# One burst for each group's norm pieces in layer 1 of a hybrid decoder step

## The chip, the cores and the metric

The kernel runs on one core of one Trainium2 chip. The metric is the device time of one execution in microseconds. Three runs of the kernel before gave 1513.77, 1514.11 and 1514.53 us (median 1514.11). Engines: PE is the matmul engine (PEld its weight loads), DVE the vector engine, ACT the scalar engine, POOL the GpSimd engine, SP the engine that issues most transfers.

## The reference

One inference step of two layers for a prompt of 1024 tokens with 16 meta tokens ahead of it and for 8 sample tokens. Model width is 1024. Layer 0 mixes tokens by gated linear attention (4 heads), layer 1 by a Mamba-2 scan (32 heads in 4 groups of B and C, a causal convolution over 4 rows). Each layer normalises its input, projects it, mixes, gates, projects back, normalises and adds:

```
for i in range(DEPTH):                       # DEPTH = 2
    h = rmsnorm(x, pre_norm[i])
    if i % 2 == 0: y, S = gla_mixer(h, ...)      # h @ w_in (1024 x 3088), chunked scan, @ w_out
    else:          y, S, buf = ssd_mixer(h, ...) # h @ w_in (1024 x 5152), conv, chunked scan, @ w_out
    x = x + rmsnorm(y, post_norm[i])
```

Everything is float32. The outputs are the two results and the new states.

## The kernel before

**Tiles.** The 1048 token columns are cut into nine steps: step 0 holds the 24 sample and meta columns, steps 1 to 8 hold 128 tokens each. Group 0 is steps 0 to 4, group 1 is steps 5 to 8. A layer's heads are cut into four units u. A matmul in float32 precision is made of three products of high and low halves, so each weight tile is converted twice: its high half by ACT (`high`, line 867 or 876), its low half by DVE (`low`, line 883 or 885).

**Two kinds of work.** The mixing of a unit's step (`distance`, `keys`, `levels`, `decay`, `state`, `attend`, `scale`, `products` and others in layer 0; `scan`, `gates`, `norm`, `inputs`, `products`, `sample` and others in layer 1) is a chain through PE, ACT and DVE. The projections of units to come are *pieces*: one piece is 24 matmuls (line 1482) over 268 or 512 columns, cut into four parts of six. A piece's bank is evacuated by ACT (`evac`) and emptied by DVE (`drain`) where two results are made from it. Pieces use three banks in turn: piece i waits until piece i - 3 has been drained.

**Norm pieces.** Before a group's first unit in a layer, the normalised rows must stand as columns in `h`. Each step of the group has two norm pieces, each with four transposes (line 1114). ACT writes the high half of `h` from the bank (line 1492), DVE the low half (line 1540). Before them stand `n_in` (the rows' load), `n_square` (ACT and POOL) and `n_scale` (DVE, line 1078). In layer 1, group 0 has ten norm pieces (108 to 117) and group 1 has eight (202 to 209). The next piece after them is a `low` one, which waits until the two banks before it are free.

**The order.** `Plan` writes one list of tasks, and every engine runs its own tasks of it in that order. `skeleton` lists the mixing steps with `fill` entries between them and a `mark` at each unit's first load. `fill_in` places the pieces: between two marks it takes the cost that has to be placed (`goal`), divides it by the sum of the fills and places parts until the spent cost reaches the due share (`pieces_to`). A piece costs its columns / 128; a norm piece costs 1.2. With a piece's first part go the `evac` of the piece before it and `finish`, `close` and `store` of earlier ones; with its second part the `drain` of the piece before it (`part`). In the order before, pieces 106 to 111 lie between mark 6 and mark 7 (unit (0, 1, 3)), 112 to 117 behind it. The steps around them are those of layer 0, group 1, units 1 and 2, as (u, s): a step is named here by the event whose `keys` it holds. Pieces 202 to 205 lie ahead of mark 11 (unit (1, 0, 3)) and 206 to 209 behind it, in the steps of layer 1, group 0, unit 2.

Of the kernel before, what the change touches and what calls it, by code (L numbers as in the profile page):

```python
# [94 lines left out]
class Piece:  # L95
# [18 lines left out]
    @property  # L114
    def cost(self):
        if self.tile >= 0:
            return CGS[self.g][1] / P
        return 1.2 if self.kind == "norm" else 0.6


class Plan:


    def __init__(self):
        self.pieces, self.tiles = [], []
        self.last = []
        self.early, self.low = {}, {}
        for L, G, u in UNITS:
            self.unit(L, G, u)
            self.last.append(len(self.pieces) - 1)  # L130
        self.first_of = {}
        self.last_of = {}
        for i, p in enumerate(self.pieces):
            if p.tile >= 0:
                self.first_of.setdefault(p.tile, i)
                self.last_of[p.tile] = i
        self.weights, self.order, self.lows = [], [], []
        self.at = (0, 0)
        self.fill_in(self.skeleton())

    def unit(self, L, G, u):
# [209 lines left out]
    def lag(self, i, names):  # L351
        if 0 <= i < len(self.pieces):
            for name in names:
                self.order.append((name, i))

    def store_lag(self, i):

# [48 lines left out]
        return whole + (self.pieces[i].cost * p / self.pieces[i].parts if p else 0.0)  # L406

    def pieces_to(self, cost):
        while self.at[0] < len(self.pieces) and self.spent(self.at) < cost - 1e-6:
            self.part()  # L410

    def goal(self, k):
        return self.spent((min(self.last[k] + 5, len(self.pieces)), 0))

    def fill_in(self, tasks):

        marks = [i for i, t in enumerate(tasks) if t[0] == "mark"]
        assert [tasks[i][1] for i in marks] == list(range(len(UNITS)))
        for i, task in enumerate(tasks):
            if task[0] == "mark":  # L420
                self.pieces_to(self.goal(task[1]))
                if task[1] + 1 < len(UNITS):
                    end = marks[task[1] + 1]
                    room = sum(t[1] for t in tasks[i:end] if t[0] == "fill")
                    base = self.spent(self.at)
                    rate = (self.goal(task[1] + 1) - base) / room
                    filled = 0.0
                else:
                    rate = 0.0
            elif task[0] == "fill":  # L430
                if rate:
                    filled += task[1]
                    self.pieces_to(base + rate * filled)
            elif task[0] == "weight":
                self.high(("out", task[1]))
            elif task[0] == "lows":
                self.low_now()
            else:
                self.order.append(task)


# [2347 lines left out]
```

## Time and profile before

| | |
|---|---|
| median of three runs | 1514.11 us |
| profiled execution | 1509.73 us |
| its span | 1508.0 us |
| mean granted PE clock | 0.983 |
| PE busy | 1416.8 us (94%) |
| DVE busy | 1166.0 us (77%) |
| ACT busy | 837.3 us (56%) |
| POOL busy | 241.6 us (16%) |

All rows come from the profiled execution. Times of rows are microseconds from the start of its span. A busy share is an average over stretches with different limits; PE's busy time counts a matmul that runs at half clock in full.

### The profile page before, as it was taken

The page shows a single profiled execution, that of the slowest core. Times are in us where ns is not written, and L with a number is a line of the kernel's source. Part 1 is how long each engine was busy: PE and PEld are TensorE (multiplying, and loading weights), DVE is VectorE, ACT ScalarE, POOL GpSimd, SP SyncE. Part 2 cuts the span into 40 slices and gives each one's busy share as a digit, 9 for nine tenths or more (in the row PEclk, how much of TensorE's full clock was granted, in tenths as well). Part 3 has the DMA queues.
Part 4 walks back from the last instruction along what each step waited for, and adds up shares of the span by engine and source line. Part 5 has one row for each costly group of instructions (what it writes and reads, how often), then busy time and mean ns, then how long its engine had stood idle before and what let it go on. Part 6 is the DMA issues. An engine that isn't in the chain of part 4 may idle for free. (4 is left out here: it accounts for less than half of the span.)

```text
span 1508.0 us, 31302 instructions
## 1 busy us (share of the span) xinstructions
PE 1416.8 (94%) x11554; PEld 1179.1 (78%) x11554; DVE 1166.0 (77%) x2591; ACT 837.3 (56%) x1877; POOL 241.6 (16%) x424
## 2 busy tenths in 40 slices
PE   5989999799999969999999999989999999999987
PEld 5889887667888759898888988867777777777765
DVE  4556587758877887968977898995889787588786
ACT  4745555356556545546655665664655556465453
POOL 5010122001332100012111112121011211000002
PEclk8999999999999999999999999999999999999999
DMA  6465557355585433448844764753485574555453
GB/s 191 126 217 145 173 171 220 96 164 165 150 202 182 128 117 108 140 107 214 251 128 125 237 200 145 212 160 98 144 264 163 152 212 131 161 155 174 139 190 63
DMA packets 283874, 245.77 MB, mean 163 GB/s; under 512 B 32664, under 2 KB 250876, under 8 KB 283052
## 3 DMA queue, kind: packets, MB, share of 16 engines
q1 hardware_dynamic: 273628, 209.36, 47.1%
q0 software_dynamic: 10096, 34.41, 8.7%
q8 instruction: 93, 1.52, 0.4%
q14 instruction: 57, 0.47, 0.1%
HBM read 183.02 MB, written 65.00 MB: 164 GB/s over the span
## 5 line engine op out<-in xcount | busy, mean ns | idle before, releaser
L1482 PE MATMUL bank<-h,w 128*128 128x268 f32 (+1 forms) x4752 | 834.9, 330 | 22.8 <-ACT w L867 16.0
L1482 PEld LDWEIGHTS bank<-h,w 128*128 128x128 f32 x4752 | 701.5, 192 | 100.4 <-issue 25.5
L883 DVE TENSOR_TENSOR w<-w_raw,w 128x1024 fp32r<-128x1024 f32 x132 | 160.9, 1219 | 37.7 <-ACT w L867 37.2
L852 PE MATMUL bank<-s_w_out,s_yt_hi 128*128 128x512 f32 (+2 forms) x544 | 168.1, 398 | 2.0 <-DVE s_ys L2600 1.7
L867 ACT ACTIVATE w<-w_raw 128x1024 fp32r<-128x1024 f32 x132 | 138.7, 1051 | 7.3 <-DMA w_raw<-in_ssd_w_in_dram 7.3
L1560 DVE SCALAR_TENSOR_TENSOR conv<-before_conv,cw,conv 128x260 f32<-128x260 f32 (+2 forms) x216 | 125.3, 580 | 4.3
L852 PEld LDWEIGHTS bank<-s_w_out,s_yt_hi 128*128 128x128 f32 (+2 forms) x544 | 95.9, 180 | 28.4 <-issue 2.5
L852 PE MATMUL bank<-g_w_out,g_ot_hi 128*128 128x512 f32 (+2 forms) x288 | 97.2, 426 | 1.1 <-DVE g_ot_lo L2118 0.9
L852 PE MATMUL bank<-s_w_out,s_yt_lo 128*128 128x512 f32 x240 | 94.7, 395 | 0.0
L2363 ACT ACTIVATE s_decay<-s_decay,t_ac 128x128 f32<-128x128 f32 (+1 forms) x288 | 85.5, 379 | 1.2
L1528 ACT ACTIVATE conv<-bank,cw 128x268 f32<-128x268 f32 (+1 forms) x72 | 45.8, 637 | 72.2 <-PE bank L1482 55.3
L2682 ACT ACTIVATE s_yt_hi<-bank 128x512 fp32r<-128x512 f32 (+1 forms) x36 | 20.1, 557 | 110.7 <-PE bank L2673 110.6
L1813 POOL TENSOR_SCALAR g_omean<-g_osum 128x1 f32<-128x1 f32 (+1 forms) x36 | 17.0, 471 | 387.2 <-ACT squares L2090 387.1
L2338 POOL TENSOR_SCALAR s_ymean<-s_ysum 128x1 f32<-128x1 f32 (+1 forms) x36 | 18.4, 510 | 363.9 <-ACT squares L2666 363.7
L2321 POOL DMA_DIRECT2D out_dram<-s_sample_state x32 | 25.1, 784 | 301.8 <-DVE s_sample_state L2475 301.8
L1632 DVE SCALAR_TENSOR_TENSOR stage<-stage,conv 128x268 f32<-128x268 f32 (+1 forms) x72 | 37.3, 519 | 41.5 <-ACT stage L1589 41.1
L852 PEld LDWEIGHTS bank<-g_w_out,g_ot_hi 128*128 128x128 f32 (+2 forms) x288 | 52.9, 186 | 18.9 <-DVE g_ot_lo L2118 2.9
L1851 ACT ACTIVATE g_decays<-g_decays 128x1024 f32<-128x1024 f32 (+1 forms) x36 | 35.2, 979 | 57.2 <-DVE g_decays L1839 57.2
L1901 ACT ACTIVATE g_vr_turned<-bank 128x512 f32<-128x512 f32 (+1 forms) x36 | 21.2, 590 | 73.7 <-PE bank L1889 73.7
L2563 PEld LDWEIGHTS bank<-s_xdt,s_decay 128*32 128x32 f32 (+1 forms) x2112 | 33.7, 109 | 27.3 <-issue 27.3
L1520 ACT ACTIVATE conv<-bank 128x268 f32<-128x268 f32 (+1 forms) x72 | 32.6, 453 | 38.8 <-PE bank L1482 34.4
L2175 DVE SCALAR_TENSOR_TENSOR y_acc<-bank,s_yrstd,y_acc 128x512 f32<-128x512 f32 (+1 forms) x54 | 39.2, 745 | 19.1 <-PE bank L852 19.0
(259 smaller groups left out, 2458.8 us busy)
## 6 DMA issues: line engine op xcount, KB each, us to landing
w_raw<-in_ssd_w_in_dram SPq DMA_DIRECT2D x80, 512.0 KB, 4.3
w_raw<-in_gla_w_in_dram SPq DMA_DIRECT2D x48, 512.0 KB, 4.5
s_decay<-kept_acd SPq DMA_DIRECT2D x32, 512.0 KB, 6.3
w_raw<-in_ssd_w_out_dram SPq DMA_DIRECT2D x30, 512.0 KB, 4.1
g_chunk<-kept_gq SPq DMA_DIRECT2D x32, 448.0 KB, 5.2
s_chunk<-kept_sq SPq DMA_DIRECT2D x32, 384.0 KB, 4.9
kept_sq<-stage SPq DMA_DIRECT2D x80, 134.0 KB, 4.4
kept_sq<-stage SPq DMA_DIRECT2D x40, 256.0 KB, 4.8
```

What stands on the lines that cost most here:

```text
L852: last = pe.matmul(bank[0:r, :], yt[a][:, k, 0:r], wo[:, b, 512 * half:512 * half + 512], start=(k + a + b == 0), stop=(k == tiles - 1 and ...
L867: act.activation(self.part(i, 0), self.raw(i), ACT.Copy).then_inc(self.w_hi, 1)
L883: dve.tensor_tensor(self.part(i, 1), self.raw(i), hi, ALU.subtract).then_inc(self.w_lo, 1)
L1482: last = pe.matmul(bank[:, 0:n], w[:, p.tile % 2, a, k, :], h[:, b, k, c:c + n], start=(i == 0), stop=(i == len(terms) - 1))
L1520: act.activation(self.work(i)[:, 0:n], bank[:, 0:n], ACT.Tanh, scale=0.5).then_inc(self.tanhed, 1)
L1528: act.activation(self.work(i)[:, 0:n], bank[:, 0:n], ACT.Identity, scale=m["cw"][:, 3, a:a + 1], bias=m["cw"][:, 4, a:a + 1])
L1560: return dve.scalar_tensor_tensor(out=u[:, off:n], in0=x[:, k:k + w], scalar=cw[:, k, a:a + 1], in1=u[:, off:n], op0=ALU.mult, op1=ALU.add)
L1632: dve.scalar_tensor_tensor(out=self.slot(i)[:, 0:n], in0=self.slot(i)[:, 0:n], scalar=1.0, in1=self.work(i)[:, 0:n], op0=ALU.add, op1=ALU. ...
L1851: act.activation(E, E, ACT.Abs).then_inc(self.dabs, 1)
L2175: return dve.scalar_tensor_tensor(out=y, in0=bank, scalar=rstd, in1=y, op0=ALU.mult, op1=ALU.add)
L2363: last = act.activation(L[0:n, r, :], L[0:n, r, :], ACT.Relu, scale=-1.0, bias=ac[0:n, s, h:h + 1])
L2563: last = pe.matmul(self.own(u, s)[rows, r * HD:(r + 1) * HD], G[0:n, r, rows], t["xdt"][0:n, r * HD:(r + 1) * HD], start=True, stop=True)
```

## The change

Norm pieces of layer 1 cost nothing in the planner. `pieces_to` stops in front of them. A new function `norms` places all norm pieces of a group one after another, and right behind them the `evac` and `drain` of the last one, which `lag` then leaves out in their old place. `fill_in` calls it at every mark and ahead of each step's first task (`distance` in layer 0, `decay` in layer 1), and it acts only when the next piece is a norm piece of layer 1. Layer 0's norm pieces keep cost and place.

```diff
     def cost(self):
         if self.tile >= 0:
             return CGS[self.g][1] / P
-        return 1.2 if self.kind == "norm" else 0.6
+        if self.kind == "norm":
+            return 0.0 if self.L else 1.2
+        return 0.6
...
+        self.drained = set()
...
     def lag(self, i, names):
         if 0 <= i < len(self.pieces):
             for name in names:
-                self.order.append((name, i))
+                if (name, i) not in self.drained:
+                    self.order.append((name, i))
...
     def pieces_to(self, cost):
-        while self.at[0] < len(self.pieces) and self.spent(self.at) < cost - 1e-6:
+        while self.at[0] < len(self.pieces) and self.spent(self.at) < cost - 1e-6 and not self.norm_next():
             self.part()
+
+    def norm_next(self):
+        p = self.pieces[self.at[0]]
+        return p.kind == "norm" and p.L == 1
+
+    def norms(self):
+
+        if self.at[0] == len(self.pieces) or not self.norm_next():
+            return
+        while self.norm_next():
+            self.part()
+        i = self.at[0] - 1
+        self.lag(i, ["evac", "drain"])
+        self.drained.update({("evac", i), ("drain", i)})
...
             if task[0] == "mark":
                 self.pieces_to(self.goal(task[1]))
+                self.norms()
...
             else:
+                if task[0] == "distance" or task[0] == "decay" and task[1] == 1:
+                    self.norms()
                 self.order.append(task)
```

## Rows read from the trace of the kernel before

**Rows 1.** The page: busy time by engine; a group: busy, mean ns, idle before.
```profile
PE 1416.8 (94%) x11554; PEld 1179.1 (78%) x11554; DVE 1166.0 (77%) x2591; ACT 837.3 (56%) x1877; POOL 241.6 (16%) x424
...
L883 DVE TENSOR_TENSOR w<-w_raw,w 128x1024 fp32r<-128x1024 f32 x132 | 160.9, 1219 | 37.7 <-ACT w L867 37.2
```

**Rows 2.** Windows of group 0's place: length, busy by engine, PE clock, DMA share, GB/s.
```profile
505.93:517.28 11.35, 11.35 (x105) 9.19 (x103) 10.49 (x25) 6.59 (x15) 2.59 (x5) 1.00 0.34 94
517.28:529.24 11.96, 10.96 (x99) 8.01 (x97) 11.10 (x26) 5.12 (x10) 0.74 (x2) 1.00 0.40 114
529.24:542.45 13.21, 8.02 (x92) 6.11 (x91) 12.34 (x27) 6.30 (x13) 1.91 (x2) 0.97 0.51 130
542.45:553.74 11.29, 8.74 (x91) 6.47 (x89) 9.26 (x26) 4.48 (x12) 0.74 (x2) 0.88 0.57 194
553.74:572.38 18.64, 14.39 (x124) 12.63 (x125) 14.25 (x32) 8.18 (x17) 0.74 (x2) 0.82 0.21 61
```

**Rows 3.** Waits of PE from 500 to 570 us: total, times, longest.
```profile
PE bank L1114 <- DVE h L1540: 5.1, 2, 3.8
PE bank L2072 <- DVE g_attn L1996: 3.4, 1, 3.4
PE bank L1482 <- ACT w L867: 1.6, 1, 1.6
```

**Rows 4.** Waits of PE from 960 to 1020 us, group 1's place.
```profile
PE bank L1482 <- ACT w L867: 3.9, 1, 3.9
PE bank L2553 <- issue: 2.5, 1, 2.5
```

**Rows 5.** Windows before and across group 1's norm pieces.
```profile
834.50:994.50 160.00, 154.40 (x1387) 134.89 (x1387) 145.14 (x366) 96.65 (x256) 30.42 (x48) 1.00 0.67 200
...
999.99:1024.68 24.69, 19.69 (x154) 15.45 (x154) 20.19 (x58) 14.26 (x43) 5.82 (x9) 0.93 0.37 97
```

**Rows 6.** Timeline of PE: start, duration, instruction, count, idle before and releaser.
```profile
496.32 4.44 PE L1482 MATMUL bank<-h,w 128*128 128x512 f32 x18
...
554.98 0.75 PE L1114 MATMUL bank<-ident,y_acc 128*128 128x128 f32 x4 [3.75 <-DVE h L1540]
...
560.73 1.04 PE L1114 MATMUL bank<-ident,y_acc 128*128 128x128 f32 x8
...
565.43 3.99 PE L1482 MATMUL bank<-h,w 128*128 128x268 f32 x18 [1.62 <-ACT w L867]
...
582.48 7.65 PE L1482 MATMUL bank<-h,w 128*128 128x268 f32 x60
```

**Rows 7.** Timeline of DVE in the same stretch.
```profile
537.07 1.28 DVE L885 SCALAR_TENSOR_TENSOR g_w_out<-w_raw,wn,g_w_out 128x1024 fp32r<-128x1024 f32 x1
...
562.41 1.89 DVE L1540 TENSOR_TENSOR h<-bank,h 128x512 fp32r<-128x512 f32 x3 [1.17 <-ACT h L1492]
```

**Rows 8.** Timeline of ACT: evacuations of norm pieces.
```profile
561.78 1.57 ACT L1492 ACTIVATE h<-bank 128x512 fp32r<-128x512 f32 x3
```

**Rows 9.** Timeline of PE at the kernel's start, layer 0's norm pieces.
```profile
11.82 1.97 PE L1114 MATMUL bank<-ident,y_acc 128*128 128x128 f32 x8 [3.07 <-DVE y_acc L1078]
...
20.38 1.97 PE L1114 MATMUL bank<-ident,y_acc 128*128 128x128 f32 x8 [2.27 <-DVE h L1540]
...
24.24 11.96 PE L1482 MATMUL bank<-h,w 128*128 128x268 f32 x75 [0.95 <-ACT cw L770]
```

**Rows 10.** Timelines of PE and DVE at the transposes of z.
```profile
1004.02 0.63 PE L2643 MATMUL bank<-ident,s_z 128*128 128x128 f32 x4 [0.45 <-DVE states L2588]
...
1006.31 1.28 DVE L1540 TENSOR_TENSOR h<-bank,h 128x512 fp32r<-128x512 f32 x2
```

**Rows 11.** The page's transfers: count, KB each, us from issue to landing.
```profile
s_decay<-kept_acd SPq DMA_DIRECT2D x32, 512.0 KB, 6.3
...
kept_sq<-stage SPq DMA_DIRECT2D x80, 134.0 KB, 4.4
```

## The prediction

> **What bounds the kernel now.** I read the page first: the matmul engine (PE) is busy for 94% of the span, the vector engine (DVE) for 77% [rows 1]. So time can only come from PE's idle 91 us and from stretches at the lower clock. Next, the windows cut at the steps' borders around group 0's norm pieces: five steps of layer 0 from 505.9 to 572.4 us, 66.5 us long [rows 2]. The reader is to compare the columns PE and DVE with the length. In the first both are full (11.35 and 10.5 of 11.35); in the next two DVE works 11.1 of 12.0 and 12.3 of 13.2 us and sets the length. In the last three PE works only 8.0, 8.7 and 14.4 us, because hardly anything but norm pieces is left to fill them, and the granted clock is 0.97, 0.88 and 0.82. PE's idle time over the five is 13.0 us; the clock adds (1 - clock) x length = 0.4 + 1.4 + 3.4, about 5 us. Third, what PE waited for there [rows 3]: norm transposes for drains (5.1), the attend matmul for DVE (3.4), the first projection after the norms (1.6; its last drain ended just before it). At group 1's place the first projection after the norms waited 3.9 and a scan 2.5 us [rows 4]; from 1000.0 to 1024.7 us PE idled 5.0, at a clock of 0.93, which is 1.7 more [rows 5]. The stake is 13 + 5 + 2.5 + 5 + 1.7 = 27 us at most. Outside these two places PE is nearly always full, and work brought forward out of those stretches is saved.
>
> **Where the pieces go.** I followed the planner's rules. A layer 1 norm piece now costs 0 instead of 1.2, so goals after each group's norms fall by 12.0 and then by 9.6 more. Between mark 6 and mark 7 the fills (24 of 0.5) have 8.0 to place instead of 12.8: one 512-column part (cost 1.0) on every third fill. The nine parts still open go 3, 2, 2, 2 over the four steps (before: 4, 3, 2, 0), and the last is placed before the last but one fill. Then the ten norm pieces stand ahead of the distance of the fifth step, with their n_scale, evacuations and drains. The next interval places 55.6 over 18.0 at a rate of 3.09 (before 3.49, of which 7.2 was for norms), so that fifth step gets 2.5 x 3.09 = 7.7, fifteen 268-column parts instead of 3. For group 1, 33.5 instead of 38.3 goes over 16.56: the last part falls in the last fill, and the eight norm pieces stand at the mark, after the transposes of z and ahead of the load for the last unit. The instructions themselves are all kept: 72 transposes, 18 evacuations, 18 drains, every weight load. Only their order changes, so this is all about waits. One more thing to read off: group 1's burst does not stand in front of a step but inside one, since its last part comes too late for the step's head.
>
> **Prices.** A 512-column part is 6 of the 18 matmuls that take 4.4 us: 1.42 us. A 268-column part is a tenth of the 60 that take 7.65: 0.75 us [rows 6]. A drain is 0.6 us (three in 1.89), an output weight's low half, and n_scale with it by its like size, 1.2 without the overlap of 0.08 [rows 7], an input weight's 1.1 [rows 1]; an evacuation 0.5 [rows 8]. A layer 0 step without extras costs DVE 9.1 us: the fourth window has 9.3 us of work, 0.9 of it drains, and each step has a wait of 0.7 for ACT that stays (10.5 of 11.35 filled) [rows 2]. For PE such a step is 11.45 - 4 x 1.42 = 5.8 us by the first window's length, in which it never idles.
>
> **Group 0.** DVE's extras per step, in the new order: 2.3 (n_scale, one low half), 0, 5.3 (n_scale, two output halves, one input half, one drain), 0. So DVE asks 11.4, 9.1, 14.4, 9.1. PE asks 5.8 + 2 x 1.42 = 8.6, and with the order of keys, parts and attend about 9.5 between two attends. The steps take 11.4 + 9.5 + 14.4 + 9.5 = 44.8, and 1.8 for the clock after the long wait that the third step leaves: 46.6 us. The third step is the weak place: nearly all extras meet in it, and PE will idle some 5 us there, as now.
>
> The burst: DVE is free about when PE is, because its add of the products ends 1 us after them and PE has a part in between. n_scale takes 1.2, the drain of piece 107 comes at +1.3, and the third norm piece needs that piece's bank. From there the drains follow at 0.6, two of them small. With three banks the round trip PE 0.5, ACT 0.5, DVE 0.6 and the handovers just fit. PE leaves the burst after 6.5 us, of which 4.3 are its own transposes: 2.2 us idle. The last two drains hide beneath keys and levels of the step (1.6 us), ahead of the low piece that waits for them. What queues behind the drains on DVE is the step's distance, 7 us late, and behind it ACT's decays. Its cover is fifteen parts, 11.3 us of PE work; without it the burst would cost those 7 us. So burst and step take 6.5 + 5.8 + 11.3 = 23.6, and 1.5 for the clock after the transposes. That last is a bound by a neighbour: the 18 matmuls after the present norms took 3.99 us where the rate of the 60 gives 2.3 [rows 6]. Zero would be the lower end, and the 2.3 us that the start of the kernel lost (75 in 11.96 instead of 9.6) the upper [rows 9].
> Sum: 46.6 + 23.6 + 1.5 = 71.7 us against 66.5, but with twelve more parts done, 9.0 us: a gain of 3.8, rounded to 4. Bounds: +9 if the third step's extras spread, -1 if the burst's round trips take 1.1 us each.
>
> **Group 1.** When PE has turned z (1004.0) DVE still has scan work until 1006.3 [rows 10]. The third norm piece waits for the drain of 201 behind it: idle 1.4. Then 1.1 in the round trips and 1.4 until the low piece's two drains: 3.9 us, in place of 7.1 (the scan's 2.5, and 5.0 of the window less 0.4 that stays) [rows 4, 5]. The clock loss stays. Against this stands that the parts moved here, eight of 0.75 us, come from earlier steps; from 834 to 994 us DVE works 145 of 160 us [rows 5], so about a third of these 6 us frees nothing there. Gain 7.1 - 3.9 - 2 = 1.2, taken as 1. Bounds: +4 if all of it is freed, -3 if the burst has the start's prices. The load of the last unit now waits for the store of piece 201, issued only inside the burst: 4.4 us, then 6.3 for the decay rows [rows 11], so these are there some 12 us after the burst begins to drain. ACT needs them after about 14 us. I take 0; if it is late, each us counts once.
>
> **The sum.** 4 + 1 = 5 us off the profiled execution's 1509.7 (span 1508.0): 1504.7. The median of the runs lies 4.4 us above that execution, at 1514.1, so I forecast 1509.0 us.
>
> **A rule against it.** At the kernel's start, where norm pieces run nearly alone, eight transposes take 1.97 us [rows 9]; at 560.7 us the same eight take 1.04 [rows 6]. The first are at 1.2 GHz, the second at 2.4, and what PE did before the first was to wait 2.3 us. The Trainium skill, "TensorE: Matmul & The Clock Gate", section "A second HAM failure mode: psum-queue depth-cycling", says that going round PSUM banks with many short idles can make the clock swing, and that throughput is lost between bursts though single matmuls look normal. The trace agrees in kind (clock 0.82 and 0.88). By that rule the burst is the wrong form; what it would do here is the second rival.
>
> **The rivals.**
> Nothing (24%): DVE bounds these steps and its work is unchanged. It works 57.4 of 66.5 us [rows 2]. PE's new parts then only push its idle time to the next step, and conv drains come onto DVE earlier. Gain of 0 to 3: about 1513.
> Slower (23%): the burst runs at the start's prices. From 11.8 to 22.3 us eight full norm pieces took 1.3 us each, mostly at 1.2 GHz [rows 9]. Then group 0's burst takes 8 x 1.3 + 0.9 = 11.3 instead of 6.5 (+4.8), group 1's 10.4 instead of 7.4 (+3.0), and each restart loses 0.7 more (+1.4): 9.2 against a gain of 5, so 1518. It decides from the point where the two bursts idle PE 5 us longer than the forecast's 2.2 and 3.9. For it: the present drains already hold PE up for 3.8 us at once (at 554.98) [rows 6]. Against it: that wait came because steps' work stood between the drains.
> More (11%): the third step's extras find room in the light steps beside it and both restarts keep the clock: +5 in group 0, +3 in group 1, 1501.
> Forecast (42%): its own range 1506 to 1511.
>
> **How the numbers follow.** A change of 0.2% (3 us) is about what can be told from none here. Faster takes nearly all of the forecast's 42% and the 11%: 0.51. Same takes the rest of these and most of the nothing case: 0.27. Slower: 0.22. The range 1502 to 1518 leaves out half of the large gain and the worst of the slower case.
>
> **What would show it.** In the new trace: nine 512-column parts spread 3, 2, 2, 2; ten norm pieces in one stretch of 6 to 7 us near 551 us, and eight in one of 7 to 8 near 1003; PE idle of 2 and 4 us in them; a wait of some 5 us on g_attn after the step with the output weights; the granted clock in the fifth step above 0.9. Wrong if a burst lasts over 10 us, if the step after it waits for distance, or if PE's idle only turns up in the steps ahead of the burst.

## The result, and the profile after: 0.65% slower

The changed kernel takes 1521.9 us (median of four runs, 1521.1 to 1523.4) against 1513.9: ratio 1.0065, 95% interval 1.0048 to 1.0082, so 7 to 12 us slower where 5 us faster was forecast. Measured again later (e15 below) it is 1.0065 again, 1.0051 to 1.0079. One execution of all, the profiled one of e5, ran at a granted clock of 0.75 and took 1743.3 us; it is left out.

The page of the changed kernel, answering to [rows 1]. Line numbers are those of before plus 21.

```profile
PE 1427.1 (94%) x11554; PEld 1184.5 (78%) x11554; DVE 1165.3 (77%) x2591; ACT 838.4 (55%) x1877; POOL 237.1 (16%) x424
...
L904 DVE TENSOR_TENSOR w<-w_raw,w 128x1024 fp32r<-128x1024 f32 x132 | 160.8, 1218 | 35.5 <-ACT w L888 35.0
```

The same 11554 matmuls keep PE busy for 10.3 us longer than before; PE's idle time in the span of 1521.6 us grew by 3.3 us, from 91.2 to 94.5. DVE does the same work. The mean granted clock is 0.976 where it was 0.983, and (1 - clock) x span is 36.5 us against 25.6, so in this execution the longer busy time is the lower clock. That is no fixed part of the loss: e15, the same kernel once more, has 5.6 us more busy and 4.6 us more idle time than before at a mean clock of 0.983, the same as before's. Both executions are slower than before by more than the medians are, since the profiled execution of the kernel before (1509.7) is a fast one.

Windows of the changed kernel around group 0's burst, one for each step of layer 0, cut where a step's first transposes of the values start on PE; columns as in [rows 2], whose cuts lie at other points of the steps, so that the rows are not to be compared one by one.

```profile
519.61:528.64 9.03, 8.94 (x92) 6.96 (x91) 8.18 (x25) 4.32 (x9) 0.99 (x2) 1.00 0.29 82
528.64:545.13 16.49, 11.88 (x93) 8.71 (x91) 14.35 (x30) 6.73 (x11) 0.74 (x2) 0.79 0.65 203
545.13:564.13 19.00, 17.18 (x162) 14.30 (x161) 15.90 (x35) 10.46 (x21) 1.06 (x2) 1.00 0.20 57
564.13:583.34 19.21, 19.21 (x188) 18.18 (x187) 14.25 (x43) 13.31 (x28) 0.74 (x2) 1.00 0.31 90
583.34:611.31 27.97, 24.13 (x250) 22.14 (x249) 23.85 (x63) 11.23 (x30) 1.99 (x2) 0.88 0.45 129
```

The third of these holds the burst: PE is busy for 17.2 of its 19.0 us at the full clock. The fourth is full. The fifth, the second step after the burst, is where it goes wrong: 28.0 us, with DVE at work for 23.9 of them and a clock of 0.88. The timeline of PE shows the burst itself (start, duration, instruction, count, idle before):

```profile
547.04 0.67 PE L1135 MATMUL bank<-ident,y_acc 24*128 24x24 f32 x8
548.52 1.53 PE L1135 MATMUL bank<-ident,y_acc 128*128 128x128 f32 x12 [0.81 <-DVE stage L1570]
550.59 1.85 PE L1135 MATMUL bank<-ident,y_acc 128*128 128x128 f32 x12 [0.54 <-DVE h L1561]
552.66 1.26 PE L1135 MATMUL bank<-ident,y_acc 128*128 128x128 f32 x8 [0.22 <-DVE h L1561]
```

It lasts 6.7 us (forecast 6.5) and PE idles 1.6 us in it (forecast 2.2). Group 1's burst in the same view, with the first projections behind it:

```profile
1010.51 0.60 PE L1135 MATMUL bank<-ident,y_acc 128*128 128x128 f32 x4
1012.30 1.60 PE L1135 MATMUL bank<-ident,y_acc 128*128 128x128 f32 x12 [1.19 <-DVE stage L1570]
1014.37 1.85 PE L1135 MATMUL bank<-ident,y_acc 128*128 128x128 f32 x12 [0.47 <-DVE h L1561]
1016.43 0.65 PE L1135 MATMUL bank<-ident,y_acc 128*128 128x128 f32 x4 [0.21 <-DVE h L1561]
1018.70 4.58 PE L1503 MATMUL bank<-h,w 128*128 128x512 f32 x12 [1.61 <-ACT w L888]
```

PE's waits in the changed kernel from 500 to 575 us, then from 575 to 640, then from 890 to 1110 us (columns as in [rows 3]):

```profile
PE bank L2093 <- DVE g_attn L2017: 4.7, 2, 3.8
...
PE bank L1135 <- DVE stage L1570: 0.8, 1, 0.8
PE bank L1135 <- DVE h L1561: 0.8, 2, 0.5
```

```profile
PE bank L1503 <- ACT t_ac L1359: 3.1, 1, 3.1
PE bank L1503 <- ACT w L888: 2.5, 1, 2.5
PE bank L1503 <- ACT before_conv L1553: 0.8, 1, 0.8
```

```profile
PE bank L2664 <- DVE states L2609: 4.5, 2, 2.9
PE bank L2574 <- issue: 3.9, 2, 2.8
PE bank L2664 <- DVE s_yt_lo L2712: 3.2, 1, 3.2
PE bank L1503 <- ACT w L888: 1.6, 1, 1.6
```

Of the 5.1 us on norm drains of [rows 3] 1.6 are left (both rows of L1135), and of the 3.9 of [rows 4] 1.6. The wait of a scan there has only moved: from 890 to 1110 us it was 4.6 us in all before and is 3.9 (L2574). New are t_ac (602 us), states (4.5 us ahead of group 1's burst, where before had 0.5) and s_yt_lo (1064 us, behind it).

To see where time is lost when the order of the work differs, I compare the two timelines at equal progress: the start of the same step on PE, less the projection work already done ahead of it (1.43 us per 512-column part, 0.43 us per norm piece). Positive is behind the kernel before:

| at (us of before) | 496 | 582 | 604 | 757 | 894 | 987 | 1034 | 1074 | end |
|---|---|---|---|---|---|---|---|---|---|
| changed | -1.0 | -7.0 | +1.0 | +4.8 | +4.8 | +11.5 | +7.3 | +13.7 | +13.3 |
| e15, changed again | -0.9 | -8.0 | +1.0 | +3.9 | +3.9 | +11.2 | +5.5 | +10.7 | +10.2 |
| e16, one evacuation | -0.2 | -7.3 | -4.3 | -0.3 | -0.3 | +6.4 | +2.3 | +8.6 | +8.4 |
| e3, old places | -1.8 | -4.0 | -2.5 | -2.2 | -2.2 | -1.0 | -5.0 | -5.0 | -4.5 |
| e12, rate behind group 1 | -1.2 | -3.6 | -3.6 | -1.6 | -1.6 | -0.3 | -2.6 | +2.6 | +3.0 |
| e7, thin before group 1 | -0.8 | -0.3 | -0.3 | +2.4 | +2.4 | +9.2 | +4.6 | +7.3 | +7.0 |
| e18, group 0's rates, one evacuation | -0.4 | -6.3 | -3.2 | -0.2 | -0.2 | +1.2 | -2.7 | -2.7 | -0.8 |

The changed kernel gains 6 us up to 582 and 4 from 987 to 1034: these are the bursts. It loses 8 from 582 to 604 and 4 more to 757, 7 from 894 to 987, and 6 from 1034 to 1074: these are stretches of projections. Each row is one execution, set against one execution of before that was 4 us faster than its median, so the last column runs high. e3, e7 and e12 have the same order up to 894 us and differ there by up to 4.6 us, so a step of this table under 3 us proves nothing, and the medians below decide.

### The profile page after: what moved, and what is told of

The parts are those of the page before. It is cut to its first block and busy times, and to the rows that moved or that the text cites. A ratio compares the mean times of both kernels' runs of the same rounds, so it can differ in the third digit from the quotient of the medians.

```text
span 1521.6 us, 31302 instructions
## 1 busy us (share of the span) xinstructions
PE 1427.1 (94%) x11554; PEld 1184.5 (78%) x11554; DVE 1165.3 (77%) x2591; ACT 838.4 (55%) x1877; POOL 237.1 (16%) x424
## 5 line engine op out<-in xcount | busy, mean ns | idle before, releaser
L2359 POOL TENSOR_SCALAR s_ymean<-s_ysum 128x1 f32<-128x1 f32 (+1 forms) x36 | 17.2, 479 | 368.9 <-ACT squares L2687 368.8
L873 PEld LDWEIGHTS bank<-s_w_out,s_yt_lo 128*128 128x128 f32 x240 | 45.3, 189 | 10.7
```

The lines of the kernel that those rows point to most:

```text
L873: last = pe.matmul(bank[0:r, :], yt[a][:, k, 0:r], wo[:, b, 512 * half:512 * half + 512], start=(k + a + b == 0), stop=(k == tiles - 1 and ...
```

## The experiments

Theory A: the bursts gain; what loses is where the re-rated projections now fall among the steps. Theory B: the burst itself costs, through the backlog it leaves on DVE and ACT. All ratios are to the kernel before on the same chip, with 95% intervals; a thousandth is 1.5 us. Each ratio rests on 4 to 12 executions of the run.

**e1 and e2, one group each.**

```diff
-            return 0.0 if self.L else 1.2
+            return 0.0 if (self.L, self.G) == (1, 0) else 1.2    # e2: (1, 1)
-        return p.kind == "norm" and p.L == 1
+        return p.kind == "norm" and (p.L, p.G) == (1, 0)         # e2: (1, 1)
```

> The change for group 0 alone; group 1's norm pieces keep cost 1.2 and their old treatment. Theory A (the bursts gain, the projections given other rates around them lose): before the change plus 4 to 7 us, since at equal progress the changed kernel was 4.8 us behind when group 0's interval was over (757 us) and stayed so until 894 us; burst near 547 us of 6 to 7 us, and the lost time behind it, at 590 to 740 us. Theory B (the burst itself costs, through DVE and ACT falling behind): the same total, but then the loss lies inside and right behind the burst, in the steps from 547 to 582 us. If group 0 costs nothing alone, the whole loss is group 1's.

> The change for group 1 alone; group 0's norm pieces keep cost 1.2 and their old treatment. Theory A: before plus 6 to 10 us (8.5 is what the changed kernel lost from 894 us on), of it about 6 ahead of the burst, where the projections are thinner, and 6 behind it, at 1034 to 1074 us, with 4 gained in the burst. Theory B: the loss in the burst and right behind it, none ahead of it. If the two groups' parts don't add up to the change's 8, the clock or an alignment of both couples them.

Measured: e1 1.0018 (1.0008 to 1.0027), e2 1.0035 (1.0023 to 1.0048). The parts, 2.7 and 5.3 us, add up to 8 of the 9.8 within their intervals. Both groups lose, and both less than I expected of them alone (4 to 7 and 6 to 10).

**e3, the bursts alone.** Norm pieces keep the cost 1.2 and are skipped where they stood; they are issued in a burst at the change's two places. Every projection stands where it stood before.

```diff
-            return 0.0 if self.L else 1.2
+            return 1.2
+        if piece.kind == "norm" and piece.L == 1 and not self.bursting:
+            self.at = (i + 1, 0)
+            return
...
+                if task == ("distance", 0, 2, 8):
+                    self.norms(0)
+                if task[1] == 11:       # at the mark
+                    self.norms(1)
```

> Both bursts stand where the change puts them, with their evacuations and drains, but every other piece (projections above all) stands exactly where it stood before the change. Theory A: the bursts' gains stay (6 and 4 us at equal progress) and most of the losses go, though the last steps ahead of each burst now have nothing to fill them: before minus 5 to plus 1 us. Theory B: before plus 6 to 10 us, as with the change.

Measured: 0.9975 (0.9964 to 0.9986), 3.8 us faster than before. Theory B is out: the same bursts at the same places gain when the projections stay. In the table group 1's burst gives 4 us of it (987 to 1034); group 0's has given nothing by 757 us (-1.8 to -2.2).

**e4, another phase.** The count of filled cost starts at 0.25 behind marks 7 and 11.

```diff
-                    filled = 0.0
+                    filled = 0.25 if task[1] in (7, 11) else 0.0
```

> The changed kernel, but in the two intervals behind the bursts' marks (7 and 11) the count of filled cost starts at 0.25 instead of 0, so that each projection part falls up to half a fill earlier; the bursts are the same. Theory A in its sharp form (what loses is only where single parts fall against the steps' waits): a time that differs from the changed kernel's by 3 us or more, either way. A systematic loss (the rates themselves, whatever the offset): within 2 us of the changed kernel. Theory B: the same as the changed kernel.

Measured: 1.0047 (1.0032 to 1.0063), 2.5 us less than the changed kernel, between the two expectations. Its profile shows why the total says little: at equal progress it was at -1.6 where the changed kernel was at +4.8 (757 us), and at -0.6 against +13.7 at 1074 us; but then it lost 8 us between 1213 and 1258 us, where the changed kernel lost half a microsecond. ACT stood still there for a transfer:

```profile
1229.53 0.37 ACT L1533 ACTIVATE conv_rows<-bank 11x256 f32<-11x256 f32 x1 [5.43 <-DMA out_dram<-conv_rows]
...
1244.87 1.06 ACT L888 ACTIVATE w<-w_raw 128x1024 fp32r<-128x1024 f32 x1 [4.62 <-DMA w_raw<-in_ssd_w_in_dram]
```

The evacuation waits until its buffer's last store has landed. It does so in the changed kernel too, for 3.6 us; moved earlier by half a fill it holds ACT up for 5.4 us, the load of a weight behind it for 4.6, and PE then waits 4.9 us for that weight, where the changed kernel waits 0.2. So in these two executions half a fill moves group 0's interval by 6 us one way and a stretch of layer 1 by 8 the other: single places decide.

**e5 and e16, one instruction moved.** Piece 126 is a short piece of transposes; its last part stood ahead of the next step's distance and decay, its evacuation (t_ac) behind them.

```diff
+        if p + 1 == piece.parts and i == 126:
+            self.lag(i, ["evac"])
+            self.drained.add(("evac", i))
```

> The changed kernel with one instruction moved: the evacuation of piece 126 (t_ac) stands right behind its transposes on ScalarE, not behind the next step's decay, where PE waited 3.0 us for it at 602 us and the clock was 0.81 to 0.93 until 625 us. Theory A (single places where a piece falls against a step's wait): the wait goes, and with it the low clock behind it; at equal progress 4 to 6 us less at 631 us, and 3 to 5 us less at the end. The rival (the steps are bound by VectorE's work, the wait only shows where PE is held up): the same time as the changed kernel within 1.5 us, with the wait back at another line within the same two steps.

> The changed kernel once more, on the chip of e16: 1.0055 to 1.0075 of before by its first four runs.

> e5 once more (its profile was not usable): the changed kernel with the evacuation of piece 126 ahead of the step's decay. If the one wait of 3.0 us on t_ac and the low clock behind it are worth what e5 and the changed kernel differ by (2.5 thousandths, 3.8 us): 2.5 to 5 us under e15, with PE's wait at 602 us gone and the granted clock from 580 to 620 us above 0.95. If their difference was that of the chips: within 1.5 us of e15.

e5 gave 1.0040 (1.0027 to 1.0053), 3.8 us under the changed kernel. Side by side on one chip, e15 gave 1.0065 (1.0051 to 1.0079) and e16 1.0030 (1.0019 to 1.0041): 5.3 us for one instruction (4.5 by the medians, 1520.9 and 1516.4), where 2.5 to 5 were expected. The timeline of ACT in the changed kernel shows the queue:

```profile
595.89 0.30 ACT L1870 ACTIVATE g_ebcum<-g_chunk 128x128 f32<-128x128 f32 x1
599.63 1.06 ACT L1872 ACTIVATE g_decays<-g_decays 128x1024 f32<-128x1024 f32 x1 [3.43 <-DVE g_decays L1860]
600.71 1.06 ACT L1874 ACTIVATE g_decays<-g_decays 128x1024 f32<-128x1024 f32 x1
...
602.25 0.25 ACT L1359 ACTIVATE t_ac<-bank 128x128 f32<-128x128 f32 x1
```

ACT waits 3.4 us for DVE's distance, does two decays, and only then empties the bank for which PE has been waiting (second line: PE's timeline there):

```profile
595.74 3.75 PE L1503 MATMUL bank<-h,w 128*128 128x268 f32 x17
602.55 1.47 PE L1503 MATMUL bank<-h,w 128*128 128x268 f32 x6 [3.06 <-ACT t_ac L1359]
```

With the evacuation ahead of the decay the wait is gone. Windows from 580 to 620 us, first of e15, then of e16:

```profile
580.00:620.00 40.00, 36.15 (x377) 33.47 (x376) 32.93 (x84) 18.51 (x47) 2.73 (x4) 0.87 0.32 94
```

```profile
580.00:620.00 40.00, 39.23 (x420) 36.80 (x419) 37.42 (x100) 18.89 (x48) 3.27 (x4) 0.96 0.44 123
```

PE has 3.1 us more of work time and the clock gives back (0.96 - 0.87) x 40 = 3.6 us. The clock was low ahead of the wait already, in both kernels: in the changed one the 24 matmuls from 594.8 us on, ahead of the wait, took 4.72 us, and in e16 these and six more took 5.47, where the 7.65 us for 60 of [rows 6] give 3.1 and 3.8. What the wait added is the second low stretch, behind it. The rival, that the wait would come back at another line in the same steps, fell for this window: 377 matmuls became 420. Just behind it some of it did come back: e16 waits 3.6 us for a weight's high half at 620.7 us (e15 2.5), the clock is low behind that, and its lead over e15 at equal progress goes from 5.3 us at 604 to 4.2 at 757.

**e6 and e8, every evacuation at once.** The same edit with the condition `piece.L == 1 and piece.kind != "norm"`, on the changed kernel (e6) and on e3 (e8).

> The changed kernel with every evacuation of a layer 1 piece right behind its last part, so that no step's decay, conv or scale stands between a part and its evacuation. Theory A: all waits of PE's banks for ScalarE that a step's work causes go (5.1 us on w excepted, that is another line): 3 to 8 us less than the changed kernel. The rival: no difference beyond 2 us, or slower, because ScalarE now waits for a part's end ahead of the step's own work.

> e3 with every evacuation of a layer 1 piece right behind its last part. If the step's work between a part and its evacuation costs PE waits in the old places too (1.3 us on before_conv in group 0 there): 1 to 4 us less than e3, so 5 to 8 us less than before. If not: e3 within 2 us.

Measured: e6 1.0090 (1.0077 to 1.0103), e8 1.0043 (1.0027 to 1.0058): 3.8 and 10.3 us slower than the kernels they came from. A gain was expected of both; e6's rival had "slower", but through ACT waiting for the end of a part, and e8 fell outside both of its expectations. Both lose 7 us between 1213 and 1258 us through conv_rows, as e4 did. The timeline of ACT in e8:

```profile
1228.62 0.37 ACT L1544 ACTIVATE conv_rows<-bank 11x256 f32<-11x256 f32 x1 [5.14 <-DMA out_dram<-conv_rows]
...
1243.13 1.06 ACT L899 ACTIVATE w<-w_raw 128x1024 fp32r<-128x1024 f32 x1 [3.79 <-DMA w_raw<-in_ssd_w_in_dram]
```

The evacuation's late place is right where it has something to wait for, and wrong where a waiting decay stands ahead of it.

**e7 and e10 to e12, the rates interval by interval.** On e3, norm pieces cost 0 only in chosen intervals, so these have the change's projections and all others the old ones: marks 10 to 11, ahead of group 1 (e7); 6 to 8, around group 0 (e10); 7 to 8 (e11); behind mark 11 (e12).

```diff
-            return 1.2
+            return 0.0 if self.L and Piece.free else 1.2
...
+                Piece.free = task[1] in (10,)     # e10: (6, 7), e11: (7,), e12: (11,)
```

> As e3 (both bursts, all projections in their old places), but in the interval ahead of group 1's norm pieces (marks 10 to 11) the projections go at the change's lower rate. The accounting of the changed kernel and of e2 says that steps of layer 1 ahead of the burst lost 5 to 6 us at equal progress since they got thinner without getting shorter; behind the burst the parts that were done late are the old ones again. If that is so: e3 plus 3 to 6 us. If only single alignments count: e3 within 2 us, or either way.

> e3 with the change's rates in the intervals around group 0's burst (marks 6 to 7 and 7 to 8), group 1 as in e3. Group 0 alone cost 2.8 us over before (e1) where e3 gained 3.6 with both bursts; if the parts of the decomposition add up: e3 plus 3 to 6 us (1.0000 to 1.0015 of before). If the rates of group 0 cost nothing and e1's loss came from group 1's untouched norms standing in a disturbed order: e3 within 1.5 us.

> e3 with the change's lower rate only in the interval behind group 0's burst (marks 7 to 8), the parts ahead of it in their old places. The time at equal progress puts group 0's loss behind the burst (12 us from 582 to 757 us of the changed kernel, after 6 gained): if it is this rate, this kernel has e10's loss, e3 plus 3 to 6. If it is the spreading ahead of the burst (fewer parts in the first steps), this kernel is e3 within 1.5 us and e10 has the loss.

> e3 with the change's lower rate only in the interval behind group 1's burst (marks 11 to 12). In the changed kernel 6 us were lost there at 1034 to 1074 us (a new wait of 3.2 us on s_yt_lo and the low clock behind it); with half a fill's offset (e4) they were not. If the rate is to blame: e3 plus 4 to 6 us. If it was the place of one part: e3 within 2 us, either way.

| | ratio | 95% interval | over e3, us |
|---|---|---|---|
| e7 | 1.0033 | 1.0020 to 1.0046 | +8.8 |
| e10 | 0.9998 | 0.9988 to 1.0009 | +3.5 |
| e11 | 1.0001 | 0.9992 to 1.0010 | +3.9 |
| e12 | 1.0009 | 1.0000 to 1.0018 | +5.1 |

Group 0's loss is all behind the burst (e11 has it whole; the 3, 2, 2, 2 ahead of it costs nothing). Group 1's largest term, 8.8 us, is above the 3 to 6 I expected: the thinner steps ahead of it. (The table has 7 us of it behind 894 us; 4.6 more stand ahead of that, where e3 and e7 have the same order.) These are their windows, steps 4 of unit 1 and 0, 1, 2 of unit 2, in e3 and then in e7:

```profile
891.93:913.47 21.54, 19.44 (x183) 16.83 (x182) 20.75 (x60) 12.21 (x38) 4.99 (x9) 1.00 0.39 124
913.47:943.68 30.21, 30.21 (x205) 26.48 (x203) 23.83 (x55) 14.65 (x42) 3.55 (x7) 1.00 0.39 119
943.68:966.27 22.59, 21.63 (x207) 18.27 (x206) 21.32 (x57) 15.58 (x41) 4.01 (x7) 1.00 0.72 223
966.27:986.11 19.84, 17.65 (x178) 16.14 (x176) 19.16 (x47) 12.80 (x31) 3.92 (x6) 0.91 0.96 273
```

```profile
896.56:919.08 22.52, 19.67 (x172) 15.79 (x171) 21.69 (x63) 12.33 (x38) 4.99 (x9) 0.92 0.46 139
919.08:947.84 28.76, 28.76 (x193) 25.02 (x191) 19.89 (x45) 12.87 (x38) 2.03 (x7) 1.00 0.42 129
947.84:970.79 22.95, 20.01 (x189) 16.72 (x188) 22.04 (x60) 15.33 (x39) 4.37 (x8) 0.96 0.59 181
970.79:990.99 20.20, 17.33 (x177) 15.45 (x177) 19.27 (x47) 12.96 (x32) 3.91 (x6) 0.96 0.85 246
```

By the placement e7 has 1.5, 1.5, 2.2 and 0 us less projection work in them, 5.2 in all. Only the second, in which PE never idles, got shorter, by 1.45 us. The first and third have DVE at work for 96 and 94% of their length in e3; they got longer, by 1.0 and 0.4 us. Together 94.4 us against 94.2: nothing was freed, and the 5.2 us of work then stand elsewhere. What took their place is 3.4 us more of idle time (8.7 against 5.3) and 1.7 us more of (1 - clock) x length (3.5 against 1.8); PE waits there for the scan's states (2.9 and 1.6 us). By its trace e12's loss is one wait and the clock behind it: PE stands 3.2 us for s_yt_lo, as in the changed kernel, e3 has no such wait, and the table has the loss between 1034 and 1074. No edit of that one place was run. The terms of group 1 do not add up: e3's gain of 3.8 and the losses 3.5, 8.8 and 5.1 would make 13.6, the changed kernel has 9.8. What the thin interval leaves undone moves every place behind it.

**e13 and e14, is it DVE?** On e3, one DVE instruction of a step (s_xdt) executed three times.

```diff
+        for _ in range(2 if (u, s) in ((1, 4), (2, 1), (2, 2)) else 0):    # e14: (0, 6), (0, 7), (3, 2)
+            self.link(dve, dve.tensor_tensor(xdt, X, dt, ALU.mult))        # operands shortened
```

> e3 with one VectorE instruction of a step (s_xdt, 0.68 us) executed three times instead of once in three steps ahead of group 1's norms (unit 1 step 4, unit 2 steps 1 and 2), where VectorE is busy 20.8 of 21.5, 21.3 of 22.6 and 19.2 of 19.8 us; the result is the same, VectorE has 4 us more to do. If VectorE sets the length of these steps, so that thinner projections could not shorten them: e3 plus 3 to 5 us. If PE sets it (busy 19.4, 21.6 and 17.7 us of them): e3 plus at most 1.5.

> The same 4 us of additional VectorE work in three steps in which PE is always busy (unit 0 steps 6 and 7, unit 3 step 2; VectorE 16.1 of 21.0, 21.1 of 24.3 and 16.9 of 24.0 us). The control to e13: e3 within 1 us if VectorE's own time is what counts there and the room beside PE takes it; e3 plus 3 to 5 if any lengthening of the chain inputs to scan costs, wherever it stands.

Measured: e13 0.9998 (0.9986 to 1.0009), e3 plus 3.5 us; e14 0.9987 (0.9977 to 0.9998), e3 plus 1.8. The intervals overlap, and in the traces the three steps grew by 1.1, 1.5 and 0.0 us in e13, by 1.0, 0.8 and 0.7 in e14, of 1.4 added to each. So the control failed: work added to a layer 1 step on DVE lengthens it also where PE looks full. That DVE's sheer amount of work sets the length of the steps ahead of group 1 is not shown. What is shown is that three of the four did not get shorter with less projection work (e7) and that two of three got longer with more on DVE (e13). What in the chain from inputs to scan is late stays open.

**e9 and e17, bursts where the projections end.** If the old rates are kept, group 0's projections end in the third of the five steps and group 1's ahead of its last, and PE idles in the steps after (in e3 it is busy for 8.8 of 13.7 and 13.1 of 18.0 us of group 0's last two). e9 puts each burst there, ahead of the next distance or decay, and works out the rate anew up to the second mark ahead. e17 starts that count at 0.75 for group 0 and moves a finished piece's evacuation ahead of a layer 0 decay (pieces 127 and 134).

```diff
-            return 0.0 if self.L else 1.2
+            return 1.2
...
+                    self.norms()                       # ahead of a distance or decay, once the parts are done
+                    to = min(now + 2, len(UNITS) - 1)
+                    room = sum(t[1] for t in tasks[i:marks[to]] if t[0] == "fill")
+                    base = self.spent(self.at)
+                    rate = (self.goal(to) - base) / room
+                    filled = 0.0                       # e17: 0.75 if now == 6 else 0.0
...
+                done = self.at[0] - 1                  # e17 only
+                if task[:2] == ("decay", 0) and done > 117 and self.at[1] == 0:
+                    self.lag(done, ["evac"])
+                    self.drained.add(("evac", done))
```

> The norm cost stays 1.2, so the projections ahead of each group's norms keep their old places and end in the third of the five steps; the burst stands ahead of the next step's distance (group 0: the fourth step, group 1: ahead of the decay of the last step before mark 11), and the rate is worked out anew from there to the second mark ahead, so that the steps that e3 left empty get 4.2, 7.9 and 5.0 of projection cost. Theory A: in e3 PE was busy 8.8 of 13.7 us and 13.1 of 18.0 us in the fourth and fifth step of group 0 and 18.2 of 21.7 us in group 1's step; filling these 13 us by half gives e3 minus 3 to 7 us, so before minus 6 to 11. The rival (these steps are bound by VectorE, which gets the pieces' drains on top): e3 within 2 us, or slower by up to 5 as the bursts meet the step with the output weights.

> e9 with the pieces behind group 0's burst placed 0.75 of a fill earlier, and with the evacuation of a piece that is done ahead of a layer 0 decay moved ahead of it (pieces 127 and 134). In e9 PE waited 5.2 us at 591.8 us for the evacuation of piece 125, whose last part stood just behind the decay, and the clock was 0.87 in that step. If such a piece across a decay is what the places behind a burst cost: the wait and the low clock go, e9 minus 3 to 6 us, before minus 8 to 11. If VectorE's backlog (23.0 of the 26.2 us of that step) only moves the wait: e9 within 2 us.

Measured: e9 0.9966 (0.9953 to 0.9979), 5.1 us under before, 1.4 under e3: less than expected, and not to be told from e3. Its burst meets the step with the output weights, where PE waits 5.3 us for DVE, and it has a piece across a decay again. PE's timeline of e9:

```profile
538.88 5.74 PE L1143 MATMUL bank<-ident,y_acc 128*128 128x128 f32 x28 [5.26 <-DVE stage L1578]
...
591.83 1.71 PE L1511 MATMUL bank<-h,w 128*128 128x268 f32 x6 [5.18 <-ACT before_conv L1561]
```

e17: 0.9958 (0.9944 to 0.9972), 6.4 us under before. The second wait is gone, but the total fell by 1.2 us only, against 3 to 6 expected: part of it came back as three waits for g_attn, 6.2 us from 520 to 640 us, where e9 had one of 2.2. Here the rival was nearer.

**e18, the best of both parts.** e10 with the evacuation of piece 126 moved as in e16.

> e10 (both bursts, the change's rates around group 0, group 1's projections in their old places) with the evacuation of piece 126 ahead of the decay, which took 5.3 us off the changed kernel (e16 against e15). If the terms add up: e10 minus 4 to 6 us, so 0.9955 to 0.997 of before, below e3. If e3's old places around group 0 avoid more than that one wait: between e10 and e3, 0.9975 to 0.9995.

Measured: 0.9965 (0.9952 to 0.9979), e10 minus 5.0 us, in the expected band. With that one instruction out of the way the change's rates around group 0 cost nothing against e3's old places: e18 is 1.5 us faster, but the intervals overlap. e17, e18 and e9 all beat both kernels; which of them is fastest the runs don't tell.

## Why the prediction was wrong

What held, by its own steps. The placement: nine parts 3, 2, 2, 2, ten norm pieces in a row at 547 us, eight at 1010. The third step: 16.5 us (forecast 14.4 and 1.8 for the clock), with a wait on g_attn of 3.8 us that ended at 538.9 (forecast some 5). The burst of group 0: 6.7 us (6.5), idle 1.6 (2.2), and the clock of the fifth step 1.00; the 1.5 us put down for the clock behind this burst were not lost (18 matmuls in 2.46 us). Group 1's: PE idles 1.2, 0.5, 0.2 and 1.6 us until the projections go on (forecast 3.9 in all, measured 3.5). The clock loss behind it is there in this execution, as forecast, and not in e15: the first 12 matmuls take 4.58 us in one and 3.03 in the other. The gain inside the bursts' stretches was even above forecast: 6 us against 4 in group 0, and 4 against 3.2 for group 1's burst less its waits. e3 shows a net 3.8 us in time. Two misreadings in the sums (11.45 for 11.35 in the price of a bare step, 2.3 for 2.4 at the kernel's start) change nothing.

The slower rival named the wrong mechanism: the bursts never ran at the start's prices. That goes for the Trainium skill's rule on short idles between PSUM banks too ("TensorE: Matmul & The Clock Gate", "A second HAM failure mode: psum-queue depth-cycling"): in this trace the step with group 0's burst, short idles and all, stayed at 1.00, and so did group 1's burst from 1010.5 to 1018.7 us; only the 4.4 us behind that ran at 0.61, and in e15 not even those.

The step that failed is the sum of group 0: "but with twelve more parts done, 9.0 us: a gain of 3.8". It stops at 572 us and pays for work done ahead at PE's full price, as if every later step shortened by what is taken out of it. I had read "outside these two places PE is nearly always full" from the busy share and took no account of the next interval, although the text itself said that its rate falls from 3.49 to 3.09, so that every piece up to 757 us stands elsewhere. There one evacuation landed behind a waiting decay: 5.3 us (e16 against e15), which is more than all of group 0's loss of 3.5 to 3.9 us (e10, e11). With it moved the loss is gone, but the forecast gain of 4 does not come either. In the table e16 and e18 are 7.3 and 6.3 us ahead at 582 us and 0.3 and 0.2 at 757, about as far as they were at 496: what was credited for parts done ahead was given back while the lower rate placed fewer. By the ratios e18 is 5.3 us under before, of which some 4 are group 1's burst by the table, so I estimate 1 to 2 us for group 0.

The second failed term is group 1's "about a third of these 6 us frees nothing there. Gain 7.1 - 3.9 - 2 = 1.2". Of 5.2 us of work taken out of those steps nothing was freed (e7: 94.4 against 94.2 us), and the lower rate ahead of group 1 costs 8.8 us where I had put 2. The number that should have warned me stood in [rows 5]: DVE at work for 145 of 160 us. An average of 91% hides steps at 94 to 97%, and of the four steps only the one in which PE never idled got shorter. Why the others did not is open, as said at e13 and e14. Behind the burst came one more wait (s_yt_lo, 3.2 us) that I had not looked for; the lower rate there costs 5.1 us (e12).

So the forecast's mechanism was right for the bursts, and the omission was what the change does outside them: it moved the projections of four intervals in order to move 18 pieces.

## What to carry to other kernels

When an edit frees slots in a hand-interleaved order, price the re-placed work over the whole interval it is spread on, step by step: here, taking work out paid only in the step where that engine never idled. Pin everything else and move only the burst (e3) before letting the rates follow; the difference was 13.6 us here. Then look in each in-order queue for a short instruction that frees a bank and stands behind a waiting one: moving one such evacuation was worth 3.8 to 5.3 us, as much as the two bursts (3.8), while moving all of them cost 4 to 10 us, since at least one had a transfer of its own to wait for.

## What the runs showed of the hardware

- A wait of 3.1 us cost 5.3 us (3.8 by e5): the granted clock around it was 0.87 over 40 us in e15 and 0.96 in e16. Where PE idled in pieces of 0.2 to 1.6 us, in the two bursts (1.6 us of 6.7, and 3.5 of 8.2 up to the first projection), the clock stayed at 1.00.
- The clock differs from one execution of a kernel to the next with the waits nearly unchanged. The changed kernel had a mean of 0.976 and, in e15, 0.983. Behind group 1's burst, after the same wait of 1.6 us, the same 12 matmuls took 4.58 us in one and 3.03 in the other. What the clock costs a change can't be read from one pair of traces.
- One and the same kernel spreads by 7 us over twelve runs (e3: 1505.9 to 1513.2), and two kernels with the same order up to 894 us stood 4.6 us apart there. Effects of 3 us need the medians.
